# Finish of the recurrent heads, small loads of the attention, and last rows of the last head: one change to a decoder layer step

## The chip, the cores and the metric

The kernel runs on one core of one Trainium2 chip. The metric is the device time of one execution in microseconds. Three runs of the kernel before took 2062.02, 2064.7 and 2070.59 us (median 2064.7).

## What is computed

One step of one decoder layer for 1024 prompt tokens and 32 sample tokens (8 sequences of 4), all in fp32. The part around the change, cut from the reference:

```python
o_att = attend(q, k4, v, lam)                                   # 4 heads of differential attention
o_att = (_rmsnorm(o_att, lp['g_subln']) * (1.0 - lam_init)).reshape(b, t, D_ATT)
y, wkv = _wkv_scan(wkv0.astype(f32), r_h, w_h, k_h, v_h, kk, a_h)   # 8 recurrent heads of 64
mean = jnp.mean(y, axis=-1, keepdims=True)
var = jnp.mean(jnp.square(y - mean), axis=-1, keepdims=True)
y = ((y - mean) * lax.rsqrt(var + GN_EPS)).reshape(b, t, D_RWKV)
y = y * lp['ln_x_w'].astype(f32) + lp['ln_x_b'].astype(f32)
bonus = jnp.sum(r_h * k_h * lp['r_k'].astype(f32), axis=-1, keepdims=True) * v_h
y = (y + bonus.reshape(b, t, D_RWKV)) * g
mix = jnp.concatenate([o_att.astype(x.dtype), o_rwkv], axis=-1) @ lp['w_o']
```

In the attention each head has two maps of scores; `softmax(first) - lam * softmax(second)` weighs the values. The samples attend to 1024 cached keys in 8 pages, found through a page table, and to their own new keys. After `mix` come norms, residuals, a convolutional feed-forward part and a gated embedding, none of them touched here.

## The kernel before

The program is a row of stages, each a block in which every engine has its own list of instructions; engines order themselves by semaphores, and all meet at the end of a block. The stages: the projection and preparation, the transitions of the recurrence (to 648 us), the scan of the recurrence (`rwkv_scan`, to 681), the attention (`attend`, to 942), the finish of the recurrent heads (`finish_rows`, to 1015), and the tail with the remaining products (`tail`, to the end).

**The scan** also loads q and k of head 0 (`ap_dup`) and splits them into a high and a low part (`ap_qs`, `ap_kh`, `ap_kl`) for the attention.

**The attention** walks over 32 steps `s` (4 heads of 8 query blocks of 128, P = 128, U = 32, NQ = 8); the order on each engine is written out in its loop over `s`. A step scores block `s` (`ap_sc`, L865 to L869), takes maxima on VectorE (L1016), exponentials on ScalarE (L1133), weighs the two maps (L1034), turns the weights with block `s - 2` (L893, kept by L1142) and multiplies by the values with block `s - 3` (L905; it leaves PSUM by L1152 and L1154). The eight sample sequences `n` run beside, one in four steps: their scores in three groups (L935), the combination of the two maps by a small matrix (`as_combs`, L951, after the sample's exponential L1191 and the products L1055 to L1062) and the values (L964). SP issues all loads: the page table, `ap_vin` (a head's values), `as_qkv`, `as_mask` and `as_comb` at the block's start, then the 16 pages of sequence 0 (each looked up in the table in SBUF, then loaded), then q and k of the next head at `s % 8 == 0`. These are rounded to the high part on ScalarE in steps 3 to 6 of a head (`split`, L1109) and the low parts made on VectorE in steps 4 to 7 (`low`, L1006, L1009).

After a head's last block its 8 blocks of rows (`ap_orow`) are normed: a root on ScalarE (`root_rows`, L1162), a reciprocal and a product on VectorE (`norm_rows`, L1040, L1042), transposes on TensorE (`turn_rows`, L913), a copy with the gain (`keep_rows`, L1171) and a store (L782). For the last head that follows the last step, and the samples' rows (`as_rows_out`, L1096, L995, L1100) are normed with it: one root over both.

**The finish** works on four pairs `p` of heads (128 rows: two heads of 64, by 1056 tokens). A mean is a product with a block matrix (`blk64`, 1/64 in two 64x64 blocks), which leaves the mean in every row; three matmuls of 352 columns each make a triple. Then the subtraction (`centre`, L1726), the square (L1688), the variance by the same matrix (L1679), root (L1694), reciprocal (L1730), product (L1732), scale and add (L1735, with bonus and bias; the bias is added before by GpSimd, L1771), and GpSimd multiplies by the gate (L1776). The result is rounded to a high part on ScalarE (L1698), and VectorE takes the low part (L1740). Beside it the attention's rows are split into high and low (`o_high` L1702, `o_low` L1744), and two tiles of the output weights (L1718, L1760).

**The tail** starts with matmuls of `Mh`, `Ml` with those weights (L2096).

Of the kernel before, what the change touches and what calls it, by code (L numbers as in the profile page):

```python
# [17 lines left out]
F32 = mybir.dt.float32  # L18
# [692 lines left out]
def attend(kit, a, proj, oT, ident, identb, causal, lam, eps, g_subln, dup, qs, kh, kl):  # L711
# [12 lines left out]
    names = ("table_in", "small_in", "q_zeroed", "q_placed", "w_zeroed", "v_turned", "v_kept", "scored", "moved", "peaked",  # L724
             "biased", "exped", "inverted", "scaled", "combined", "turned", "kept", "summed", "squared", "evacuated", "v_in", "normed",
# [4 lines left out]
    with ExitStack() as ctx:  # L730
        vin = kit.sb(ctx, "ap_vin", [P, SEQ])
# [11 lines left out]
        table = kit.sb(ctx, "as_table", [1, NB * PAGES], I32)  # L743
        qkv = kit.sb(ctx, "as_qkv", [P, 3, HEADS, NS])
        qd = kit.sb(ctx, "as_qd", [P, NB, HEADS, 32])
        vnew = kit.sb(ctx, "as_vnew", [NS, HEADS, P])
        mask = kit.sb(ctx, "as_mask", [P, NB * NS], BF16)
        comb = kit.sb(ctx, "as_comb", [P, 18])
# [17 lines left out]
        def _(sp):  # L766
# [8 lines left out]
            def load_v(h):  # L775
                if h:
                    sp.wait_ge(S["v_turned"], h)
                sp.dma_start(vin[:], proj[h + 2 * HEADS][:, 0:SEQ]).then_inc(S["v_in"], 16)

            def store(h):  # L780
                sp.wait_ge(S["o_kept"], h + 1)
                sp.dma_start(oT[h][:, 0:SEQ], out[:]).then_inc(S["o_stored"], 16)  # L782
# [17 lines left out]

            sp.dma_start(table[:], a["table"]).then_inc(Z["table_in"], 16)
            load_v(0)
            for j in range(3):
                sp.dma_start(qkv[:, j], proj[j * HEADS:(j + 1) * HEADS, :, SEQ:T].rearrange("h p t -> p h t"))\
                    .then_inc(Z["small_in"], 16)
            sp.dma_start(mask[:], a["new_mask"]).then_inc(Z["small_in"], 16)
            sp.dma_start(comb[:, 0:17], a["comb"]).then_inc(Z["small_in"], 16)
            sp.wait_ge(Z["table_in"], 16)
# [3 lines left out]
            for s in range(U + 3):  # L812
                h, n = s // NQ, s // 4
                if s % NQ == 0 and h + 1 < HEADS:
# [12 lines left out]
            store(HEADS - 1)  # L827
            sp.wait_ge(Z["out_kept"], 1)
            sp.dma_start(oT.rearrange("h p t -> p h t")[:, :, SEQ:T], out_s[:]).then_inc(Z["stored"], 16)
            sp.wait_ge(Z["stored"], 16)  # L830
            sp.wait_ge(S["o_stored"], 16 * HEADS)

        @block.gpsimd
        def _(pool):
            nc.gpsimd.memset(qd[:], 0.0).then_inc(Z["q_zeroed"], 1)
            nc.gpsimd.memset(wS[:], 0.0).then_inc(Z["w_zeroed"], 1)
            pool.wait_ge(Z["small_in"], 16 * 5)
# [2328 lines left out]
```

## Time and profile before

| | |
|---|---|
| median of 3 runs | 2064.7 us |
| the profiled execution | 2063.8 us, span 2062.0 us |
| TensorE matmul, weight load | 1852.0 us (90%), 1752.3 us (85%) |
| VectorE, ScalarE, GpSimd | 1078.5 us (52%), 810.7 us (39%), 292.7 us (14%) |
| granted TensorE clock, mean | 0.938 |

The span runs from the first to the last instruction; the execution's own time has 1.8 us around it. Busy time is time in which an engine executes; where several matmuls overlap their ends are modelled. In a row of the trace the number in brackets is how long the engine sat idle before, and the arrow names what it was waiting for. The granted clock is a share of 2.4 GHz: 0.50 is the lower of TensorE's two levels.

### The profile page before, as it was taken

To read this page: it belongs to the slowest core of one execution; us is meant where nothing else is said; L and a number is where in the kernel's file an instruction comes from. 1 tells how busy PE (TensorE), PEld (TensorE's weight loads), DVE (VectorE), ACT (ScalarE), POOL (GpSimd) and SP (SyncE) were. 2 spreads that over 40 slices of the span, in tenths; PEclk is the share of its full clock that TensorE was granted. 3 is DMA by queue.
4 is the path that set the end of the run, shared out by engine and by line. 5 is a ranking of instruction groups with operands and counts; after the bars stand their busy time and mean duration, and the time that the engine had idled before them with its cause. 6 is when DMAs were issued, how large, how long until landed. Compare 5 with 4: busy or idle time off the path is not lost.

```text
span 2062.0 us, 45942 instructions
## 1 busy us (share of the span) xinstructions
PE 1852.0 (90%) x19468; PEld 1752.3 (85%) x19468; DVE 1078.5 (52%) x1790; ACT 810.7 (39%) x1438; POOL 292.7 (14%) x292
## 2 busy tenths in 40 slices
PE   5999999699998588884397999999999999999996
PEld 5988888599997466662397999999999999999996
DVE  4355544345445455545736577553337766532654
ACT  4242323022232266652234554543335555432442
POOL 0011111059971000002100000000000000000000
PEclk9999999899999688886699999999999999999997
DMA  4233333530012677534133343323434422333442
GB/s 153 99 124 128 132 119 135 194 110 3 3 26 45 192 215 196 152 103 169 41 103 134 104 144 129 100 89 118 137 113 153 146 92 93 99 111 106 121 139 95
DMA packets 100140, 240.71 MB, mean 117 GB/s; under 512 B 14243, under 2 KB 18467, under 8 KB 99651
## 3 DMA queue, kind: packets, MB, share of 16 engines
q1 hardware_dynamic: 99362, 235.63, 35.9%
q8 instruction: 154, 2.52, 0.5%
q10 hardware_dynamic: 576, 2.16, 0.3%
q14 instruction: 48, 0.39, 0.1%
HBM read 189.54 MB, written 48.21 MB: 115 GB/s over the span
## 4 chain that ended last, share of the span: by engine, by line
PE 47%; DVE 2%; ACT 1%; issue 1%; DMA 0%; POOL 0%; SPq 0%; ACTq 0%; DVEq 0%
PE tl_acc L2096 45%; PE tl_ple L2096 1%; PE tl_wide L2070 0%; PE tl_wide L2061 0%; DVE tl_tmp L2369 0%; DVE tl_gated L2431 0%; DVE tl_gated L2434 0%; ACT tl_sq_e L2108 0%; ACT tl_wh L2245 0%; DVE tl_Y L2351 0%; DVE tl_Y L2342 0%; ACT tl_Hh L2214 0%; DVE tl_acc_e L2275 0%; DMA tl_xt<-dram_xT 0%; ACT tl_Y L2194 0%
## 5 line engine op out<-in xcount | busy, mean ns | idle before, releaser
L2096 PE MATMUL tl_acc<-tl_Hh,tl_wh 128*128 128x264 f32 x1536 | 438.5, 285 | 7.4 <-DVE tl_Hl L2373 7.4
L2096 PE MATMUL tl_acc<-tl_Hh,tl_wl 128*128 128x264 f32 x1536 | 438.1, 285 | 0.0
L2096 PE MATMUL tl_acc<-tl_Hl,tl_wh 128*128 128x264 f32 x1536 | 436.1, 284 | 0.0
L2415 DVE TENSOR_TENSOR tl_wl<-tl_raw,tl_wh 128x1024 fp32r<-128x1024 f32 (+2 forms) x182 | 206.0, 1132 | 418.7 <-ACT tl_wh L2245 418.5
L2245 ACT ACTIVATE tl_wh<-tl_raw 128x1024 fp32r<-128x1024 f32 (+2 forms) x182 | 178.9, 983 | 497.1 <-PE tl_acc L2096 455.9
L2096 PEld LDWEIGHTS tl_acc<-tl_Hh,tl_wh 128*128 128x128 f32 x1536 | 290.0, 189 | 8.7 <-DVE tl_Hl L2373 8.4
L2096 PEld LDWEIGHTS tl_acc<-tl_Hl,tl_wh 128*128 128x128 f32 x1536 | 290.3, 189 | 0.0
L2096 PEld LDWEIGHTS tl_acc<-tl_Hh,tl_wl 128*128 128x128 f32 x1536 | 290.1, 189 | 0.0
L2096 PE MATMUL tl_acc<-tl_Gl,tl_wh 128*128 128x264 f32 x704 | 200.4, 285 | 0.0
L2096 PE MATMUL tl_acc<-tl_Gh,tl_wl 128*128 128x264 f32 x704 | 200.3, 284 | 0.0
L2096 PE MATMUL tl_acc<-tl_Gh,tl_wh 128*128 128x264 f32 x704 | 200.1, 284 | 0.0
L2289 DVE SCALAR_TENSOR_TENSOR tl_c<-tl_u,par,tl_c 128x528 f32<-128x528 f32 (+1 forms) x176 | 136.6, 776 | 13.2 <-ACT tl_c L2161 6.6
L2096 PEld LDWEIGHTS tl_acc<-tl_Gh,tl_wl 128*128 128x128 f32 x704 | 132.7, 189 | 0.0
L2096 PEld LDWEIGHTS tl_acc<-tl_Gh,tl_wh 128*128 128x128 f32 x704 | 132.6, 188 | 0.0
L2096 PEld LDWEIGHTS tl_acc<-tl_Gl,tl_wh 128*128 128x128 f32 x704 | 132.5, 188 | 0.0
L2698 PE MATMUL fr_ps<-fr_Hh,fr_wh 128*128 128x272 f32 x416 | 124.0, 298 | 5.7 <-DVE fr_wl L2821 5.7
L2821 DVE TENSOR_TENSOR fr_wl<-fr_raw,fr_wh 128x512 fp32r<-128x512 f32 x52 | 37.0, 714 | 175.1 <-ACT fr_wh L2733 175.1
L2698 PE MATMUL fr_ps<-fr_Hl,fr_wh 128*128 128x272 f32 x416 | 121.4, 292 | 0.0
L2698 PE MATMUL fr_ps<-fr_Hh,fr_wl 128*128 128x272 f32 x416 | 121.1, 291 | 0.0
L2451 POOL COPY tl_u<-tl_carry 128x2 f32<-128x2 f32 x88 | 34.5, 392 | 603.3 <-DVE tl_conv_out L2293 355.3
L2733 ACT ACTIVATE fr_wh<-fr_raw 128x512 fp32r<-128x512 f32 x52 | 32.6, 629 | 204.0 <-PE fr_ps L2682 127.6
L2096 PE MATMUL tl_acc<-Mh,tl_wh 128*128 128x264 f32 x256 | 75.1, 293 | 28.4 <-PEq L82 27.7
(360 smaller groups left out, 4458.2 us busy)
## 6 DMA issues: line engine op xcount, KB each, us to landing
tl_raw<-dram_w_up SPq DMA_DIRECT2D x88, 512.0 KB, 3.6
as_kT<-dram_k_pool SPq DMA_DIRECT2D x64, 256.0 KB, 3.1
as_vp<-dram_v_pool SPq DMA_DIRECT2D x64, 256.0 KB, 3.0
tl_raw<-dram_w_down SPq DMA_DIRECT2D x32, 448.0 KB, 3.4
dram_projT<-fr_cur SPq DMA_DIRECT2D x26, 528.0 KB, 2.9
fr_raw<-dram_w_in SPq DMA_DIRECT2D x52, 256.0 KB, 3.6
tl_raw<-dram_w_pg SPq DMA_DIRECT2D x32, 320.0 KB, 3.2
ap_dup<-dram_projT SPq DMA_DIRECT2D x16, 512.0 KB, 8.9
```

The costliest lines, as they stand in the source:

```text
L2096: last = nc.tensor.matmul(out[:, n, 0:HP], w[:, u % 2, k, :], z, start=(begin and q == 0), stop=(end and q == 2))
L2245: nc.scalar.activation(wh[:, u % 2, 0:kt], raw[:, u % 3, 0:kt], ACT.Copy).then_inc(S["rounded"], 1)
L2289: stt(c, uu[:, k:k + n], tap(f"cw{k}", m), c, ALU.mult, ALU.add).then_inc(S[f"tap{k}"], 1)
L2415: tt(wl[:, u % 2, 0:kt], raw[:, u % 3, 0:kt], wh[:, u % 2, 0:kt].bitcast(F32), ALU.subtract).then_inc(S["residued"], 1)
L2451: ins = nc.gpsimd.tensor_copy(uu[:, 0:2], carry[:, x.m])
L2698: last = nc.tensor.matmul(accB[:, n, 0:w2b], w[:, u % 2, k, :], x[:, row, at:at + w2b], start=(row == 0 and q == 0), stop=(row == KD - 1 a ...
L2733: nc.scalar.activation(wh[:, u % 2], raw[:, u % 3], ACT.Copy).then_inc(S["rounded"], 1)
L2821: tt(wl[:, u % 2], raw[:, u % 3], wh[:, u % 2].bitcast(F32), ALU.subtract).then_inc(S["residued"], 1)
```

## The change

Four things are changed.

1. In the finish the variances are no longer spread over all 128 rows at once. A matrix `var_cols` (128x32 for each pair) sums the squares into 2 of 32 rows, all four pairs accumulate into the same rows, and the three groups of 352 tokens stand at rows 0, 32 and 64 of one PSUM bank. One root and one reciprocal work on 96x352. A matrix `var_rows` then spreads the result over the 128 rows, pair by pair, and the product reads it in PSUM. The means have two PSUM tiles instead of one. The bias moves from GpSimd to ScalarE. The loads of the attention's rows all come before bonus and gate, and VectorE's list is in another order.
2. The averaging matrix, the two new ones, and the attention's table, `qkv`, mask, `comb` and first values are loaded in the scan, behind that stage's own loads; SP waits for them there.
3. In the attention q and k of head 1 are loaded ahead of the pages of sequence 0, and the rounding and the low parts of q and k each run one step earlier in every head.
4. At the end of the attention the samples' rows have a root, reciprocal and product of their own; the last head's rows are normed as 7 blocks and 1 block, and stored so; the samples' rows are stored first.

```diff
 # rwkv_scan, SP
             sp.dma_start(yt[:], ysd.rearrange("t h a v -> t (h a v)")).then_inc(S["sample_in"], 16)
+            for dst, src in early:
+                sp.dma_start(dst, src).then_inc(S["early_in"], 16)
+            sp.wait_ge(S["early_in"], 16 * len(early))
             sp.wait_ge(S["state"], NCH)
...
 # attend, VectorE and ScalarE
-                if s % NQ >= NQ - 4 and s // NQ + 1 < HEADS:
-                    low(s // NQ + 1, s % NQ - (NQ - 4))
-            norm_rows(HEADS - 1)
+                if NQ - 5 <= s % NQ < NQ - 1 and s // NQ + 1 < HEADS:
+                    low(s // NQ + 1, s % NQ - (NQ - 5))
+            dve.wait_ge(Z["rooted"], 1)
+            nc.vector.reciprocal(rms[:, 2], rms[:, 2]).then_inc(Z["o_inverted"], 1)
...
+            norm_rows(HEADS - 1)
...
+            norm_rows(HEADS)
...
-                if h < HEADS and NQ - 5 <= i < NQ - 1:
-                    if i == NQ - 5:
+                if h < HEADS and NQ - 6 <= i < NQ - 2:
+                    if i == NQ - 6:
...
+                if s == U + 1:
+                    act.wait_ge(Z["squared"], NB)
+                    nc.scalar.activation(rms[:, 2], rms[:, 2], ACT.Sqrt, bias=eps, scale=1.0 / P).then_inc(Z["rooted"], 1)
+                    root_rows(HEADS - 1)
...
+            root_rows(HEADS)
             keep_rows(HEADS - 1)
+            act.wait_ge(S["o_turned"], HEADS + 1)
+            nc.scalar.activation(out[:, SEQ - P:SEQ], pv[:, 0:P], ACT.Copy, scale=gs[:]).then_inc(S["o_kept"], 1)
...
 # finish_rows, TensorE
+            def var(p):
+                pe.wait_ge(S["squared"], p + 1)
+                for n in range(3):
+                    last = nc.tensor.matmul(pr[group(n), 0:T3], var_cols[:, p, :], sq[:, p % 2, n * T3:(n + 1) * T3],
+                                            start=(p == 0), stop=(p == NPAIR - 1), skip_group_check=True)
+                last.then_inc(S["var"], 1)
+
+            def spread(p):
+                if p >= 2:
+                    pe.wait_ge(S["scaled"], p - 1)
+                for n in range(3):
+                    last = nc.tensor.matmul(wide[p % 2][:, n, 0:T3], var_rows[group(n), p, :], rstd[group(n), :],
+                                            start=True, stop=True)
+                last.then_inc(S["spread"], 1)
+
             mean(0)
+            mean(1)
             for p in range(NPAIR):
-                if p + 1 < NPAIR:
-                    mean(p + 1)
...
+                var(p)
+                if p + 2 < NPAIR:
+                    mean(p + 2)
+            pe.wait_ge(S["inverted"], 1)
+            pe.wait_ge(S["centred"], NPAIR)
+            for p in range(NPAIR):
+                spread(p)
...
 # finish_rows, VectorE and GpSimd
-                dve.wait_ge(S["rooted"], p + 1)
-                nc.vector.reciprocal(sd[:, p % 2], sd[:, p % 2]).then_inc(S["inverted"], 1)
-                dve.wait_ge(S["inverted"], p + 1)
-                tt(dev[:, p], dev[:, p], sd[:, p % 2], ALU.mult).then_inc(S["divided"], 1)
+                dve.wait_ge(S["spread"], p + 1)
+                tt(part(dev[:, p]), part(dev[:, p]), wide[p % 2][:, :, 0:T3], ALU.mult).then_inc(S["scaled"], 1)
...
-            for p in range(NPAIR):
-                pool.wait_ge(bon_in[p], 16)
-                nc.gpsimd.tensor_scalar(BON[:, p], BON[:, p], param("ln_b", 4)[:, p:p + 1], None, ALU.add)\
-                    .then_inc(S["shifted"], 1)
```

How instructions stand on SP around the start of the attention. `wkv_prompt` is the scan's last store, `as_kT` a page of keys, `ap_dup` q and k of a head, `rn_yt` a load of the scan. Before:

```order
L1486 DMA rn_yt<-dram_ysd 32x512
L1488 DMA dram_wkv_prompt<-rn_states 128x256
L1470 UNCONDITIONAL_BRANCH
L765 UNCONDITIONAL_BRANCH
L801 DMA as_table<-dram_table 1x64
L778 DMA ap_vin<-dram_projT 128x1024
L804 DMA as_qkv<-dram_projT 128x4x32 x3
L806 DMA as_mask<-dram_new_mask 128x256
L807 DMA as_comb<-dram_comb 128x17
L785 TENSOR_LOAD as_table
L785 ISA x2
L791 ISA
```

And in the changed kernel, from the scan's last own load to the first look-up of a page:

```order
L1492 DMA ap_vin<-dram_projT 128x1024
L1492 DMA as_table<-dram_table 1x64
L1492 DMA as_qkv<-dram_projT 128x4x32 x3
L1492 DMA as_mask<-dram_new_mask 128x256
L1492 DMA as_comb<-dram_comb 128x17
L1492 DMA rf_blk<-dram_blockmean 128x128
L1492 DMA rf_cols<-dram_var_cols 128x128
L1492 DMA rf_rows<-dram_var_rows 128x512
L1495 DMA dram_wkv_prompt<-rn_states 128x256
L1474 UNCONDITIONAL_BRANCH
L760 UNCONDITIONAL_BRANCH
L768 DMA ap_dup<-dram_projT 64x2x1024 x4
```

The small loads stand before the scan's store; the attention's list begins with the four loads of head 1, and the look-ups of the pages follow them.

VectorE in the finish, from the end of the first subtractions (`rf_dev` the deviations, `rf_sd` the spread root, `Ml` a low part). Before:

```order
L1726 TENSOR_TENSOR rf_dev<-mixed,rf_pm 128x1056 x2
L1744 TENSOR_TENSOR Ml<-rf_O,Mh 128x1056
L1730 RECIPROCAL rf_sd<-rf_sd 128x1056
L1732 TENSOR_TENSOR rf_dev<-rf_dev,rf_sd 128x1056
L1735 SCALAR_TENSOR_TENSOR rf_dev<-rf_dev,par,rf_BON 128x1056
L1726 TENSOR_TENSOR rf_dev<-mixed,rf_pm 128x1056
L1744 TENSOR_TENSOR Ml<-rf_O,Mh 128x1056
L1730 RECIPROCAL rf_sd<-rf_sd 128x1056
```

Now, from the third subtraction's low part on (`rf_rstd` the narrow rows, `rf_wide` the spread ones in PSUM):

```order
L1778 RECIPROCAL rf_rstd<-rf_rstd 96x352
L1764 TENSOR_TENSOR Ml<-rf_O,Mh 128x1056
L1752 TENSOR_TENSOR rf_dev<-rf_dev,rf_wide 128x1056
L1755 SCALAR_TENSOR_TENSOR rf_dev<-rf_dev,par,rf_BON 128x1056
L1752 TENSOR_TENSOR rf_dev<-rf_dev,rf_wide 128x1056
L1755 SCALAR_TENSOR_TENSOR rf_dev<-rf_dev,par,rf_BON 128x1056
L1768 TENSOR_TENSOR tl_wl<-tl_raw,tl_wh 128x1024
L1760 TENSOR_TENSOR Ml<-mixed,Mh 128x1056
L1752 TENSOR_TENSOR rf_dev<-rf_dev,rf_wide 128x1056
L1755 SCALAR_TENSOR_TENSOR rf_dev<-rf_dev,par,rf_BON 128x1056
L1768 TENSOR_TENSOR tl_wl<-tl_raw,tl_wh 128x1024
L1760 TENSOR_TENSOR Ml<-mixed,Mh 128x1056
```

All four subtractions now stand ahead of the one reciprocal, and the residues of the weights and the low parts stand between the scalings instead of behind them.

## Rows read from the trace of the kernel before

**Rows 1.** Windows; busy us (count) of PE, PEld, DVE, ACT, POOL; clock, DMA share, GB/s.

```profile
681.00:942.00 261.00, 196.94 (x1748) 159.82 (x1748) 132.85 (x304) 142.76 (x351) 3.26 (x10) 0.79 0.60 171
942.00:1015.00 73.00, 24.11 (x49) 12.97 (x49) 58.61 (x26) 18.67 (x18) 24.31 (x8) 0.59 0.29 112
...
718.00:720.00 2.00, 1.94 (x6) 1.66 (x7) 0.61 (x2) 2.00 (x8) 0.00 (x0) 0.50 1.05 386
```

**Rows 2.** Timeline, VectorE in the finish: start, us, engine, line, operation [idle before].

```profile
949.89 1.25 DVE L1726 TENSOR_TENSOR rf_dev<-mixed,rf_pm 128x1056 f32<-128x1056 f32 x1 [14.64 <-PE rf_pm L1667]
...
958.46 6.75 DVE L1730 RECIPROCAL rf_sd<-rf_sd 128x1056 f32<-128x1056 f32 x1 [1.01 <-ACT rf_sd L1694]
...
966.54 1.32 DVE L1735 SCALAR_TENSOR_TENSOR rf_dev<-rf_dev,par,rf_BON 128x1056 f32<-128x1056 f32 x1
...
968.94 2.67 DVE L1744 TENSOR_TENSOR Ml<-rf_O,Mh 128x1056 fp32r<-128x1056 f32 x1
...
1008.93 4.75 DVE L1740 TENSOR_TENSOR Ml<-mixed,Mh 128x1056 fp32r<-128x1056 f32 x4
```

**Rows 3.** Timeline, TensorE in the finish and at the tail's start.

```profile
945.96 3.89 PE L1667 MATMUL rf_pm<-mixed,rf_blk 128*128 128x352 f32 x6 [9.46 <-DMA rf_blk<-dram_blockmean]
...
954.83 1.94 PE L1679 MATMUL rf_pq<-rf_sq,rf_blk 128*128 128x352 f32 x6
...
1014.87 0.56 PE L2096 MATMUL tl_acc<-Mh,tl_wh 128*128 128x264 f32 x1 [27.74 <-PEq L82]
```

**Rows 4.** Timeline, ScalarE and GpSimd in the finish: a square, a gating.

```profile
951.18 1.08 ACT L1688 ACTIVATE rf_sq<-rf_dev 128x1056 f32<-128x1056 f32 x1 [13.53 <-DVE rf_dev L1726]
...
968.01 2.48 POOL L1776 TENSOR_TENSOR mixed<-rf_dev,rf_G 128x1056 f32<-128x1056 f32 x1 [4.52 <-DVE rf_dev L1735]
```

**Rows 5.** Timeline, end of the attention to the finish's first issue.

```profile
928.48 1.28 ACT L1162 ACT_TABLE_LOAD   x1
...
931.55 1.22 DVE L1096 TENSOR_TENSOR as_rows_out<-as_rows_out,ap_rms 128x1024 f32<-128x1024 f32 x1
...
932.82 1.97 PE L995 MATMUL ap_sc<-ident,as_rows_out 128*128 128x128 f32 x8 [5.11 <-DVE as_rows_out L1096]
...
934.58 1.92 PE L913 MATMUL ap_tp<-ident,ap_orow 128*128 128x128 f32 x8
...
936.54 1.11 ACT L1171 ACTIVATE ap_out<-ap_tp,ap_gs 128x1024 f32<-128x1024 f32 x1 [6.45 <-PE ap_tp L913]
...
938.05 0.43 SPq L829 DMA_DIRECT2D dram_oT<-as_out  x1
942.08 0.35 SPq L1652 DMA_DIRECT2D rf_blk<-dram_blockmean  x1
```

**Rows 6.** Loads of q and k and their first users, scan and attention.

```profile
648.10 3.12 SPq L1485 DMA_DIRECT2D ap_dup<-dram_projT  x4
...
L1516 ACT ACTIVATE ap_qs<-ap_dup x2: 1041/1049/1057, 660.9 to 661.8; 128x1024 fp32r<-128x1024 f32 x2
...
681.13 0.25 SPq L801 DMA_DIRECT2D as_table<-dram_table  x1
...
691.25 1.16 PE L935 MATMUL as_one<-as_kT,as_qd 128*32 128x384 f32 x8 [0.40 <-DVE as_vnew L1085]
...
716.17 1.06 ACT L1109 ACTIVATE ap_qs<-ap_dup 128x1024 fp32r<-128x1024 f32 x1 [14.91 <-DMA ap_dup<-dram_projT]
...
718.06 0.80 PE L865 MATMUL ap_sc<-ap_kh,ap_qs 128*128 128x512 f32 x1 [10.64 <-ACT ap_pexp L1133]
```

**Rows 7.** Timeline, TensorE at the first head change and in head 1.

```profile
739.97 0.45 PE L865 MATMUL ap_sc<-ap_kh,ap_qs 128*128 128x128 f32 x1 [4.06 <-DVE ap_kl L1009]
...
742.61 3.69 PE L951 MATMUL as_one<-as_combs,as_prob 128*128 128x16 f32 x18
...
766.70 0.54 PE L865 MATMUL ap_sc<-ap_kh,ap_qs 128*128 128x512 f32 x1 [2.14 <-ACT ap_pexp L1133]
...
771.57 2.12 PE L951 MATMUL as_one<-as_combs,as_prob 128*128 128x16 f32 x18 [1.40 <-DVE as_combs L1062]
```

More of the change, by code:

```diff
@@ L799, in values @@
                         .then_inc(Z["v_in"], 16)
[L801 to L808, printed above, removed]
+            load_qk(1)
             for g in range(3):
@@ L813, in _ @@
                 h, n = s // NQ, s // 4
[L814 removed]
+                if s % NQ == 0 and 0 < h and h + 1 < HEADS:
                     load_qk(h + 1)
@@ L911, in turn_rows @@
                 pe.wait_ge(S["kept"], min(NQ * (h + 1) + 3, U))
-                for n in range(NQ):
+                for n in range(NQ if h < HEADS - 1 else NQ - 1):
                     last = nc.tensor.transpose(tp[:, n, :], orow[:, h % 2, n, :], ident)
@@ L1624, in store, with finish_rows @@
         sp.wait_ge(state_out, 32)
-def finish_rows(kit, a, spill, oT, epsg, param, Y, Mh, Ml, raw, wh, wl):
+def finish_rows(kit, a, spill, oT, epsg, param, Y, Mh, Ml, raw, wh, wl, blk64, var_cols, var_rows):
     nc = kit.nc
-    names = ("blk_in", "mean", "centred", "squared", "var", "rooted", "inverted", "divided", "shifted", "affine", "gated", "high", "low",
+    names = ("mean", "centred", "squared", "var", "rooted", "inverted", "spread", "scaled", "shifted", "affine", "gated", "high", "low",
              "o_high", "o_low", "rounded", "residued")
@@ L1706, in _ @@
             square(1)
-            root(0)
             o_high(1)
-            root(1)
             square(2)
             o_high(2)
-            root(2)
             square(3)
-            o_high(3)
-            root(3)
+            act.wait_ge(S["var"], NPAIR)
+            nc.scalar.activation(rstd[0:ROWS], pr[0:ROWS, 0:T3], ACT.Sqrt, bias=epsg[0:ROWS]).then_inc(S["rooted"], 1)
+            o_high(HEADS - 1)
+            for p in range(NPAIR):
+                shift(p)
             for u in range(2):
@@ L1748, in _ @@
             o_low(0)
-            scale(0)
             centre(2)
             o_low(1)
-            scale(1)
             centre(3)
             o_low(2)
+            dve.wait_ge(S["rooted"], 1)
+            nc.vector.reciprocal(rstd[0:ROWS], rstd[0:ROWS]).then_inc(S["inverted"], 1)
+            o_low(3)
+            scale(0)
+            scale(1)
+            residue(0)
+            low(0)
             scale(2)
-            o_low(3)
+            residue(1)
+            low(1)
             scale(3)
-            for u in range(2):
-                dve.wait_ge(S["rounded"], u + 1)
-                tt(wl[:, u], raw[:, u], wh[:, u].bitcast(F32), ALU.subtract).then_inc(S["residued"], 1)
-            for p in range(NPAIR):
-                low(p)
-            dve.wait_ge(S["residued"], 2)
+            low(2)
+            low(3)
             dve.wait_ge(S["low"], NPAIR)
             dve.wait_ge(S["o_low"], HEADS)
+            dve.wait_ge(S["residued"], 2)
         @block.gpsimd
         def _(pool):
-            for p in range(NPAIR):
-                pool.wait_ge(bon_in[p], 16)
-                nc.gpsimd.tensor_scalar(BON[:, p], BON[:, p], param("ln_b", 4)[:, p:p + 1], None, ALU.add)\
-                    .then_inc(S["shifted"], 1)
             for p in range(NPAIR):
@@ L3101 @@
     i = np.arange(C)
+    var_cols = np.zeros((P, NPAIR, 32), np.float32)
+    var_rows = np.zeros((P, NPAIR, P), np.float32)
+    for p in range(NPAIR):
+        for h in range(2):
+            var_cols[h * C:(h + 1) * C, p, 2 * p + h] = 1 / C
+            var_rows[2 * p + h::32, p, h * C:(h + 1) * C] = 1.0
     lev = [(j[:, None] == i[None, :]) | ((j[:, None] >> (n + 1) == i[None, :] >> (n + 1))
```

128 lines of the change are left out of this document (70 added, 58 removed).

## The prediction

> **What bounds the kernel now.** I read the page first (TensorE busy nine tenths almost everywhere), then busy time by stage, then the instructions in order of time in the slack stages. The attention [rows 1] keeps TensorE 197 of 261 us busy at a mean granted clock of 0.79; the finish keeps it 24 of 73 us busy at 0.59. Every tail matmul stands behind the finish, which ends at the first tail matmul [rows 3]: what the finish or the attention loses comes off the end one for one.
>
> In the finish VectorE sets the time: it is busy 58.6 of 73 us [rows 1]. A reciprocal over 1056 elements takes 6.75 us [rows 2], and there are four: 27 us, with TensorE waiting behind them. Before that, 3.9 us pass from the block's first DMA issue [rows 5] to the first matmul, which waits for the averaging matrix [rows 3].
>
> In the attention I looked for what ended last before each long TensorE wait. 10.64 us are lost before block 5 of head 0, where ScalarE sat 14.91 us on the loads of head 1's q and k [rows 6]; 4.06 us at each of the three head changes, for the last low part of k [rows 7].
>
> **The change part by part.**
>
> *Finish, until the scaling can begin.* The block's start is t = 0 (942.1). The matrices are loaded in the scan, so the first mean runs at 0. A mean triple takes 3.9 us at the low clock; six such halves take 1.94 at the high one [rows 3]. Now two means come first, then variance and mean alternate: eight triples. I take two at the low clock (3.6 each) and five more by the 1.9 of rows 3 up to the third variance, 16.7; the last mean is done at 14.8, its subtraction (1.25) [rows 2] and square (1.08) [rows 4] at about 17.3, the last variance at 19. One square root over 96x352 replaces four over 1056 (at most the 1.08 of the square), and one reciprocal over 352 takes 6.75 x 352/1056 = 2.25. With two hand-overs the first spread matmuls start at about 21 if the narrow matmuls of 32 columns or rows share the array and the root is short, 24 if they don't. Bounds: 18.5 (clock up early, narrow ones nearly free) and 33 (all eight triples at 3.6, root, reciprocal, spread at the low clock). I take 21.
>
> The narrow matmuls of different column groups may run side by side. The Trainium skill ("TensorEngine Tiling (Array Packing)", Key Properties) says that different tiles work in parallel, but that changing the tiling mode drains the array; the finish changes it seven times. By the drain the chain would be longer by an estimated 7 x 0.3 to 0.6 us, 2 to 4 us (half a matmul of rows 3 to a whole one), and the sum would give back as much. No row here isolates that.
>
> *Finish, from there on.* VectorE has four products with the spread rows (one input in PSUM, 1.25 as the subtraction), four scale-and-adds (1.32), two weight residues (below 1.2, as one of the four low parts), four low parts (4.75/4 = 1.19) [rows 2]: 17.4 us. GpSimd has four gatings of 2.48 [rows 4]. A subtraction from SBUF took 2.67 instead of about 1.2 while a gating ran: it began at 968.94 and ended 1.1 us after the gating did [rows 2, 4]. So I put these operations one after the other, and only the products beside a gating. The order then gives, from the start of scaling: gating 0 to 5.2, scale-and-add 1 to 6.5, residue 0 to 7.6, gating 1 to 10.1, low 0 to 11.2, scale 2 to 13.8, residue 1, gating 2 and low 1 to 18.5, scale 3 to 21.0, low 2 to 22.2, gating 3 to 24.7, its rounding on ScalarE (1.08) and low 3 to 27.0. If they ran side by side, 21.4.
>
> The Trainium skill ("SBUF — State Buffer", SBUF: two separate sides) calls this an exclusive lock, taken also by a VectorE operation with two SBUF inputs, so by the scale-and-add, which no row shows beside a gating. Without it for that one the end would be 25.8 instead of 27.0.
>
> The adding of the bias moves from GpSimd (four) to ScalarE, four more at about 1.08; ScalarE is free from the root to the first gating. It is priced at nothing; should the bias or bonus loads, now behind all four attention loads in SP's queue, land after 21, scaling waits as long. The finish ends at 21 + 27.0 + 1.2 (end of the low parts to first tail matmul) [rows 2, 3] = 49.2 against 72.8 now: **23.6 us less** (11.6 to 31.7).
>
> *End of the attention.* The table load (1.28), the root, and the product of the samples' rows (1.22) now come before the last block has left, and only one block of eight is late. After 928.48 there remain: sample transposes (1.97), seven head transposes (7/8 of 1.92), copy (about 1.0), the last block's copy, SP's issue. The sample rows are stored first. I get the last issue at about 933.9 instead of 938.05 [rows 5]; the landing stays. The added wait for the samples' sums stands before the last block's square on ScalarE, and its sums are due before that. **4.2 us less** (2.5 to 5.5).
>
> *Start of the attention.* Eight small loads leave SP's queue; three more go into the scan with them. There SP waits for all of them; behind it stands only the state store, due 27 us later, so nothing. At the start, head 1's q and k (four loads, 2 MB) are now ahead of the sample pages. In the scan such loads took 660.9 - 648.1 = 12.8 us from issue to use [rows 6]. From the block's first issue at 681.13 [rows 6] that is 693.9. The first three pages (each 128x512 fp32, together 0.79 MB) at 386 GB/s [rows 1] take 2 us: the first sample scores start at 696 instead of 691.25. The order from there to block 5 is the old one (16.2 us to 707.4) plus a rounding on ScalarE and a low part on VectorE that come a step earlier, 1.2: block 5 at 713.4 instead of 718.06, **4.6 us less**. If pages overlap with the q and k loads, 7; if they land 3 us later still, 1.5.
>
> *Low parts one step earlier.* Score 8 no longer waits 4.06 us, but the next thing, the sample combination, needs the sample exponential: its matmuls at 742.61 move only to about 740.8, **1.8 us** at each of three changes. In heads 1 and 2 the earlier rounding lands between a root and an exponential that TensorE waits 2.14 us for, and the earlier low part before a combination it waits 1.40 us for [rows 7]: 1.1 + 1.0 us lost, twice. Net 1.2. If the clock then holds over the change, sample matmuls cost 2.12 instead of 3.69 [rows 7] and the value matmuls behind them gain as much: up to 3 more each. I take **3 us** (-2 to 10).
>
> **Sum.** 23.6 + 4.2 + 4.6 + 3 = 35.4. The profiled execution took 2063.8 us (span 2062.0); the median of the runs is 2064.7, 0.9 above. 2063.8 - 35.4 = **2028 us**.
>
> **The rivals.**
> *More than that:* the clock rises early and stays up over the head changes, and VectorE and GpSimd wait little. 28 + 10 + 5 + 5 = 48: 2016. For it: the gaps that let the clock fall to 0.5 shrink. Against: the 1.4 us wait for the combination stays.
> *The finish becomes bound by TensorE:* eight triples, the roots and the spread all at the low clock, and pages stuck behind q and k. 11.6 + 4.2 + 0 + 1 = 17: 2047. For it: the clock was low in the finish until 954.83 [rows 3]. Against: the triples now follow without the reciprocals between.
> *It doesn't do what it says:* the reciprocal's time doesn't shrink with its columns, or each is as late as before; under 10 us gained, about 2056.
> *Slower:* the clock in the attention. There is now one wait of nearly 10 us at its start, and TensorE is busy 197 us at a mean 0.79 [rows 1]. Were the mean to fall to x, its work would grow by 197 x (0.79/x - 1) us; from x = 0.67 that eats the 35 us, and at 0.64 the kernel takes 2028 + 46 = 2074. For it: at 718 to 720, right after the 10.64 us wait, the clock is at 0.50 [rows 1, 6]. Against: of the waits, 10.6 and 4.06 three times go.
>
> **How the numbers follow.** Forecast, 2020 to 2038: 0.62. More: 0.14. TensorE-bound finish: 0.18. Not what it says: 0.03. Slower: 0.03. The 8-in-10 range takes in parts of both neighbours: 2016 to 2042. About 0.5% (10 us) is what a measurement here tells from no change: faster 0.93, same 0.04, slower 0.03.
>
> **What would show it.** One reciprocal of about 2.25 us in the finish; its first matmul right at the block's start; 48 to 50 us from there to the first tail matmul; scale-and-adds or low parts of about 2.5 us beside the gatings. No wait of ScalarE on head 1's loads, but TensorE idle until about 696; score 8 with no wait on the low part. Last store issued some 4 us earlier, relative to the last block. The tail's length unchanged within 3 us: if not, the cause is one I did not name. The forecast is wrong if the finish takes over 60 us or the attention doesn't shorten.

## The result, and the profile after

The changed kernel took 2033.99 us (median of four runs, 2029.61 to 2034.84) against 2064.23 us in the runs of before beside it: a ratio of 0.984, 95% interval 0.982 to 0.987. Forecast were 2028 us and a range of 2016 to 2042. The profiled execution took 2033.6 us with a span of 2031.7, so 30.3 us less span than before, where the sum of the terms said 35.4. Cut by the same marks in both traces (first load of the scan, first score matmul of the attention, first DMA issue of the finish, first tail matmul):

| stage | before | after | change | forecast |
|---|---|---|---|---|
| up to the scan's first load | 648.10 | 646.39 | -1.7 | 0 |
| scan | 33.08 | 35.28 | +2.2 | 0 |
| attention | 260.90 | 254.08 | -6.8 | -11.8 |
| finish | 72.79 | 47.26 | -25.5 | -23.6 |
| tail | 1047.13 | 1048.69 | +1.6 | 0 |

Busy time by stage, the answer to [rows 1] (windows of the changed kernel: us, then busy us and count of PE, PEld, DVE, ACT, POOL, then granted clock, DMA share, GB/s):

```profile
681.62:935.75 254.13, 199.44 (x1748) 159.66 (x1748) 133.63 (x307) 143.51 (x354) 3.27 (x10) 0.81 0.59 173
935.75:983.01 47.26, 19.26 (x73) 8.62 (x73) 34.67 (x23) 19.27 (x19) 12.25 (x4) 0.61 0.44 171
```

VectorE's work in the finish fell from 58.6 to 34.7 us. The attention keeps TensorE busy 2.5 us longer than before at about the same clock: what it won, it won in waits.

The finish instruction by instruction, which answers to [rows 2 to 4] (timeline of the changed kernel: start, us, engine, line, operation, idle before and its releaser):

```profile
935.79 6.54 PE L1675 MATMUL rf_wide<-mixed,rf_blk 128*128 128x352 f32 x12 [5.04 <-PEq L82]
...
942.26 0.79 PE L1682 MATMUL rf_pr<-rf_sq,rf_cols 128*32 128x352 f32 x6
942.98 2.04 PE L1675 MATMUL rf_wide<-mixed,rf_blk 128*128 128x352 f32 x6
...
951.03 0.55 ACT L1734 ACTIVATE rf_rstd<-rf_pr,epsc 96x352 f32<-96x352 f32 x1 [0.90 <-PE rf_pr L1682]
951.62 2.35 DVE L1778 RECIPROCAL rf_rstd<-rf_rstd 96x352 f32<-96x352 f32 x1 [1.44 <-ACT rf_rstd L1734]
...
954.02 2.72 PE L1690 MATMUL rf_wide<-rf_rstd,rf_rows 32*128 32x352 f32 x12 [3.04 <-DVE rf_rstd L1778]
...
955.63 1.25 DVE L1752 TENSOR_TENSOR rf_dev<-rf_dev,rf_wide 128x1056 f32<-128x1056 f32 x1 [0.55 <-PE rf_wide L1690]
...
958.15 1.25 DVE L1752 TENSOR_TENSOR rf_dev<-rf_dev,rf_wide 128x1056 f32<-128x1056 f32 x1
958.39 2.46 POOL L1799 TENSOR_TENSOR mixed<-rf_dev,rf_G 128x1056 f32<-128x1056 f32 x1 [273.29 <-DVE rf_dev L1755]
959.44 2.52 DVE L1755 SCALAR_TENSOR_TENSOR rf_dev<-rf_dev,par,rf_BON 128x1056 f32<-128x1056 f32 x1
...
969.14 3.25 POOL L1799 TENSOR_TENSOR mixed<-rf_dev,rf_G 128x1056 f32<-128x1056 f32 x1 [3.78 <-DVE rf_dev L1755]
970.04 3.46 DVE L1760 TENSOR_TENSOR Ml<-mixed,Mh 128x1056 fp32r<-128x1056 f32 x1
...
980.61 1.26 DVE L1760 TENSOR_TENSOR Ml<-mixed,Mh 128x1056 fp32r<-128x1056 f32 x1 [3.41 <-ACT Mh L1715]
983.01 0.56 PE L2119 MATMUL tl_acc<-Mh,tl_wh 128*128 128x264 f32 x1 [22.01 <-PEq L82]
```

One reciprocal of 2.35 us stands where four of 6.75 were, and the first mean no longer waits for a load. A scale-and-add beside a gating takes 2.52 instead of 1.32 us, a low part 3.46 instead of 1.25. From the first product (955.63) to the last low part's end it is 26.2 us.

The end of the attention, the answer to [rows 5] (timeline of the changed kernel):

```profile
925.26 1.28 ACT L1215 ACT_TABLE_LOAD   x1
...
927.45 0.37 ACT L1149 ACTIVATE ap_sq<-ap_pv,ap_small 128x128 f32<-128x128 f32 x1 [0.40 <-PE ap_pv L895]
...
928.41 1.09 PE L984 MATMUL ap_sc<-ident,as_rows_out 128*128 128x128 f32 x8 [1.00 <-DVE as_rows_out L1091]
...
929.65 0.99 PE L903 MATMUL ap_tp<-ident,ap_orow 128*128 128x128 f32 x7 [0.15 <-DVE ap_orow L1034]
...
930.48 0.27 PE L988 MATMUL ap_pv<-ident,ap_orow 128*128 128x128 f32 x1
...
932.08 0.43 SPq L819 DMA_DIRECT2D dram_oT<-ap_out  x1
935.75 0.32 SPq L1661 DMA_DIRECT2D rf_O<-dram_oT  x1
```

The table load is done before the last block's square (927.45), and the transposes run at the full clock (granted 1.00 from 928.40 to 931.20; before, 0.50 from 932.82 to 936.50): 1.09 us, and 0.99 for seven blocks, instead of 1.97, and 1.92 for eight. From that square to the finish's first issue it is 8.3 us; before, it was 14.3: issue at 942.08 [rows 5], and this square (timeline of the kernel before):

```profile
927.75 0.37 ACT L1152 ACTIVATE ap_sq<-ap_pv,ap_small 128x128 f32<-128x128 f32 x1 [2.21 <-PE ap_pv L905]
```

The start of the attention and the first head change, the answers to [rows 6, 7] (timeline of the changed kernel):

```profile
681.62 2.56 SPq L768 DMA_DIRECT2D ap_dup<-dram_projT  x4
685.46 8.07 SPq L786 DMA_DIRECT2D as_kT<-dram_k_pool  x8
...
696.08 1.51 PE L924 MATMUL as_one<-as_kT,as_qd 128*32 128x384 f32 x8 [10.04 <-DMA as_kT<-dram_k_pool]
...
710.63 3.81 PE L940 MATMUL as_one<-as_combs,as_prob 128*128 128x16 f32 x18 [4.24 <-DVE as_combs L1055]
715.25 0.77 PE L854 MATMUL ap_sc<-ap_kh,ap_qs 128*128 128x512 f32 x1
...
737.82 3.82 PE L940 MATMUL as_one<-as_combs,as_prob 128*128 128x16 f32 x18 [1.74 <-DVE as_combs L1055]
...
763.65 0.64 PE L854 MATMUL ap_sc<-ap_kh,ap_qs 128*128 128x512 f32 x1 [3.09 <-ACT ap_pexp L1130]
...
769.91 3.13 PE L940 MATMUL as_one<-as_combs,as_prob 128*128 128x16 f32 x18 [2.69 <-DVE as_combs L1055]
```

The long wait at the start is now for the key pages (10.04 us), not for ScalarE. The sample combination waits at the start (4.24), at the head change (1.74) and in the middle of head 1 (2.69; before, 1.40 [rows 7]).

### The profile page after: what moved, and what is told of

Read it like the earlier page. It is cut to its first block, busy times and chain, and to the rows that moved or that the text cites. A ratio compares the mean times of both kernels' runs of the same rounds, so it can differ in the third digit from the quotient of the medians.

```text
span 2031.7 us, 45987 instructions
## 1 busy us (share of the span) xinstructions
PE 1849.8 (91%) x19492; PEld 1748.4 (86%) x19492; DVE 1051.9 (52%) x1790; ACT 812.5 (40%) x1442; POOL 280.9 (14%) x288
## 3 DMA queue, kind: packets, MB, share of 16 engines
q8 instruction: 154, 2.52, 0.5%
## 4 chain that ended last, share of the span: by engine, by line
PE 48%; DVE 2%; ACT 1%; issue 1%; POOL 0%; ACTq 0%; DVEq 0%
PE tl_acc L2119 46%; PE tl_ple L2119 1%; PE tl_wide L2084 1%; PE tl_wide L2093 1%; ACT tl_wh L2268 0%; DVE tl_tmp L2392 0%; ACT tl_sq_e L2131 0%; DVE tl_gated L2454 0%; DVE tl_gated L2457 0%; DVE tl_Y L2374 0%; DVE tl_Y L2365 0%; ACT tl_Hh L2237 0%; DVE tl_acc_e L2298 0%; ACT tl_Y L2217 0%; ACT tl_sq_x L2131 0%
## 5 line engine op out<-in xcount | busy, mean ns | idle before, releaser
L2705 PE MATMUL fr_ps<-fr_Hh,fr_wh 128*128 128x512 f32 x208 | 85.7, 412 | 14.2 <-DVE fr_Hl L2944 14.2
```

Of the source, the lines that this page charges most:

```text
L2705: last = nc.tensor.matmul(accA[:, t % 2, :], w[:, u % 2, k, :], x[:, row, 0:W_A], start=(row == 0 and q == 0), stop=(row == KD - 1 and q = ...
```

## The experiments

Single stages are compared by their traces, one for each run, with the marks of the table above. "Turn n" is the first matmul that uses the combination of sample n; turns 1, 3 and 5 follow a head change, 2, 4 and 6 lie in the middle of a head. The medians of the runs alone don't settle 3 us: the part ahead of the scan, the same code in all these kernels, took 646.4 to 656.9 us in the profiled executions. The kernel before took 2062.85 us (median) beside the first four kernels, 2064.63 beside the next four, and 2064.3 beside the rest.

**The finish alone.** The attention of before; in the scan only the finish's three matrices as early loads.

```
-            early = [(vin[:], proj[2 * HEADS][:, 0:SEQ]), (table[:], a["table"])]
...
+            early = [(blk64[:], a["blockmean"]), (var_cols[:], a["var_cols"]), (var_rows[:], a["var_rows"])]
...
-                   table, qkv, mask, comb, vin)
```

> The changed kernel's finish on the attention of before; of the early loads only the finish's three matrices are in the scan. Theory (the finish's gain is its own, and the scan's 2.2 us come from the clock at its start, not from the loads): finish, block's first issue to first tail matmul, 47.3 +-1.5 us; attention 261 +-1.5; scan 33 to 36 whatever the loads; about 2038 to 2040 us in all. Rival A (the finish is short because TensorE comes out of the changed attention at a higher clock): finish 50 us or more. Rival B (the seven loads of the attention's small inputs slow the scan): scan 33.0, as before.

Measured: finish 47.42, attention 261.54, scan 34.04 us; 2037.15 us, ratio 0.987 (0.985 to 0.989). The finish's gain is its own and needs nothing of the rest. On the scan, rival B falls: three early loads gave 34.04, and another kernel with all ten (keys first, below) 34.21. In these traces the scan's length goes with the granted clock over its first 33 us, which hold 516 matmuls (513 in the last row):

| kernel | early loads | clock | scan, us |
|---|---|---|---|
| before | 0 | 0.90 | 33.08 |
| finish alone | 3 | 0.84 | 34.04 |
| keys first | 10 | 0.84 | 34.21 |
| changed | 10 | 0.79 | 35.28 |
| changed, run again | 10 | 0.74 | 36.08 |

The traces show where the changed kernel's 2.2 us arise. The scan's first three steps take 2.10 us instead of 1.67, at a granted clock of 0.50 (649.60 to 653.80; before, 1.00 from 651 to 654): 1.3 us. The matmuls are slow from 648.51 on (1.12 us for sixteen instead of 0.68), and the first early load is issued only at 650.36, so the loads did not bring the clock down. Behind that the steps meet GpSimd's low part of q at another moment: the update of the state on VectorE, 0.42 us alone, takes 2.11 us beside it, and the one that met it before took 1.06. That is another 1.1 us. The two engines in the scan (timelines of the kernel before, then of the changed one):

```profile
662.02 4.85 POOL L1522 TENSOR_TENSOR ap_qs<-ap_dup,ap_qs 64x1024 fp32r<-64x1024 f32 x2 [56.21 <-ACT ap_qs L1516]
...
663.60 1.06 DVE L1546 TENSOR_TENSOR rn_states<-rn_tsum,ELC 128x256 f32<-128x256 f32 x1
```

```profile
660.50 4.84 POOL L1529 TENSOR_TENSOR ap_qs<-ap_dup,ap_qs 64x1024 fp32r<-64x1024 f32 x2 [56.40 <-ACT ap_qs L1523]
...
661.02 2.11 DVE L1553 TENSOR_TENSOR rn_states<-rn_tsum,ELC 128x256 f32<-128x256 f32 x1
```

Why the clock at the scan's start is lower in one execution than in another stays open; of the kernel before there is only one trace.

**The low parts at their old steps.**

```
-                if NQ - 5 <= s % NQ < NQ - 1 and s // NQ + 1 < HEADS:
-                    low(s // NQ + 1, s % NQ - (NQ - 5))
+                if NQ - 4 <= s % NQ and s // NQ + 1 < HEADS:
+                    low(s // NQ + 1, s % NQ - (NQ - 4))
...
-                    high(h, i - (NQ - 6))                 # steps 2 to 5
+                    high(h, i - (NQ - 5))                 # steps 3 to 6
```

> The changed kernel with the rounding and the low parts of the next head's k back at their old steps. My prediction: this costs 3 us (attention 257). Theory from the changed kernel's trace (what the heads gain at a change they lose again in the middle of a head, where the sample combination now comes after a low part): attention 252 to 254, that is up to 2 us faster than the changed kernel; the wait of a score matmul for the low part at a head change is back at about 4 us, and the sample combination's matmul in the middle of heads 1 and 2 comes some 29 us after the one before it instead of 32.1 and 31.1.

Measured: attention 251.37 us, 2.7 less than in the changed kernel (2032.94 us). The timeline of this kernel, the head change and head 1:

```profile
737.09 0.44 PE L854 MATMUL ap_sc<-ap_kh,ap_qs 128*128 128x128 f32 x1 [4.07 <-DVE ap_kl L1000]
...
764.78 0.50 PE L854 MATMUL ap_sc<-ap_kh,ap_qs 128*128 128x512 f32 x1 [2.14 <-ACT ap_pexp L1130]
...
769.65 3.81 PE L940 MATMUL as_one<-as_combs,as_prob 128*128 128x16 f32 x18 [2.39 <-DVE as_combs L1055]
```

The 4.07 us wait is back, yet turn 0 to turn 1 is only 0.9 us longer (28.07 against 27.19): behind the low part the combination was the next wait anyway. From turn 1 to turn 2 it is 2.2 us shorter (29.93 against 32.09), from 3 to 4 1.2 us; from 5 to 6 it is 1.1 us longer, and turn 0 comes 1.2 us earlier. So the old step is not 3 us dearer. One trace is weak for 2.7 us: the changed kernel run again (below) took 253.14. Taken over all traces here without another spacing of the low parts, the stretch from block 5's score to the last block's square is 208.6 to 210.7 us in the four with the old step (the kernel before, the finish alone, this one, and the three edits together; mean 209.7) and 210.3 to 212.6 in the six with the earlier one (mean 211.7). My term for the shift had the wrong sign: the earlier step costs some 2 us there.

**Key pages ahead of q and k.**

```
-            load_qk(1)
             for g in range(3):
                 keys(0, g)
+            load_qk(1)
             values(0)
```

> The changed kernel with the loads of head 1's q and k behind the first sample's three groups of key pages, ahead of its value pages. Theory (loads are served in the order of their issue, so what the first sample scores wait for is the 2 MB of q and k ahead of them): first sample scores 5 to 8 us after the block's first issue instead of 14.5; ScalarE then waits for q and k, some 5 us later than now; block 5's score 30 to 33 us after the block's first issue instead of 33.6, attention 251 to 254. Rival (16 DMA engines share the bandwidth, so the order of issue is worth little): first sample scores within 2 us of where they are now, block 5's score within 1 us, attention 254 +-1.

Measured: first sample scores after 6.2 us, as the theory had it; but block 5 after 36.0 us (33.6 in the changed kernel) and attention 256.25, longer by 2.2, which neither had. 2035.33 us. Its timeline:

```profile
688.19 8.07 SPq L786 DMA_DIRECT2D as_kT<-dram_k_pool  x8
696.30 2.83 SPq L768 DMA_DIRECT2D ap_dup<-dram_projT  x4
...
710.65 1.06 ACT L1106 ACTIVATE ap_qs<-ap_dup 128x1024 fp32r<-128x1024 f32 x1 [11.83 <-DMA ap_dup<-dram_projT]
```

What the theory left out are SP's issues: eight key pages take SP 8.07 us (1.0 each, the page number being read from a table first), so q and k are issued 8 us late. ScalarE starts on them 14.35 us after their first issue, and has waited 11.83 us, with everything behind it. The bytes count too: in the scan of the kernel before it was 12.8 us from issue to use [rows 6].

**The gatings on VectorE.**

```
+                dve.wait_ge(g_in[p], 16)
+                dve.wait_ge(S["affine"], p + 1)
+                tt(Y[:, p], dev[:, p], G[:, p], ALU.mult).then_inc(S["gated"], 1)
...
-                nc.gpsimd.tensor_tensor(Y[:, p], dev[:, p], G[:, p], ALU.mult).then_inc(S["gated"], 1)
```

(The second weight residue moves behind the last gating.)

> The changed kernel with the four gatings on VectorE instead of GpSimd. Theory (a gating on GpSimd and a VectorE operation of SBUF inputs shut each other out, so that a gating costs the finish its whole 2.5 us): VectorE's 18 operations from the first product on follow without a stretched one, 22.3 us from the first product to the end of the last low part instead of 26.2; finish 43 to 44 us. Rival (the two engines share SBUF only in part, and a stretched low part hides a gating): VectorE's added 4 x 1.2 us come on top of the low parts' unstretched times, 26 us or more, finish 47 us or more.

Measured: finish 43.59 us, 22.56 from the first product to the last low part; 2030.68 us. From its timeline, a gating, a low part and the last two:

```profile
967.99 1.26 DVE L1759 TENSOR_TENSOR mixed<-rf_dev,rf_G 128x1056 f32<-128x1056 f32 x1
...
979.23 1.25 DVE L1763 TENSOR_TENSOR Ml<-mixed,Mh 128x1056 fp32r<-128x1056 f32 x1
...
985.41 2.42 DVE L1763 TENSOR_TENSOR Ml<-mixed,Mh 128x1056 fp32r<-128x1056 f32 x2
```

With GpSimd silent nothing is stretched: four more operations on VectorE, and the stage is 3.7 us shorter. The two engines had taken turns in the changed kernel.

**Head 1's q and k loaded in the scan.**

```
             sp.wait_ge(S["early_in"], 16 * len(early))
+            sp.wait_ge(S["low"], 4)                       # head 0's parts are done with the buffer
+            for n in range(2):
+                ...
+                    sp.dma_start(dup[rows, n], src).then_inc(next_qk, 16)
             sp.wait_ge(S["state"], NCH)
...
-            load_qk(1)                                    # at the attention's start
```

> The changed kernel with the loads of head 1's q and k moved into the scan: SP issues them there as soon as head 0's low parts are done with the buffer, some 9 to 11 us before the attention begins, ahead of the state's store. Theory (at the start the attention loses time to two things on one queue: the 2 MB of q and k ahead of the key pages, and 1.0 us of SP per page): first sample scores 6 to 8 us after the block's first issue (14.5 in the changed kernel), ScalarE never waits for q and k, block 5's score 26 to 29 us after the block's first issue (33.6), attention 247 to 250. Rival (the loads only move: they land as late, or slow the scan's end as much): scan 5 us longer, or first sample scores after 10 us or more and attention 253 to 255.

Measured: first sample scores after 6.0 us, block 5 after 23.8 (33.6 in the changed kernel), attention 244.71; 2028.57 us. The theory was right and too small. Of the rival, half holds: the scan is 37.76 us, 2.5 longer, 2.0 of it since from the issue of the state's store, now behind the four loads, to the first score it is 4.2 us (681.15 to 685.32) instead of 2.2:

```profile
671.64 2.58 SPq L1497 DMA_DIRECT2D ap_dup<-dram_projT  x4
681.15 0.35 SPq L1499 DMA_DIRECT2D dram_wkv_prompt<-rn_states  x1
...
691.36 0.85 PE L923 MATMUL as_one<-as_kT,as_qd 128*32 128x384 f32 x8 [1.09 <-DMA as_kT<-dram_k_pool]
```

**The end of the attention undone.**

```
-                for n in range(NQ if h < HEADS - 1 else NQ - 1):
+                for n in range(NQ):
...
-                if s % NQ == 2 and NQ <= s < U:
+                if s % NQ == 2 and s >= NQ:
                     root_rows(s // NQ - 1)
...
-            norm_rows(HEADS)
...
-            root_rows(HEADS)
```

> The changed kernel with the end of the attention as before: the last head's rows normed in one part, together with the samples'. Theory (the 6.0 us between the last block's square and the finish's first issue are the code's: the table load, the root and the product no longer behind the last block): that stretch is 14.3 us again, attention 260, finish 47.3. My prediction's term: 4.2 us, attention 258.3. Rival (part of the gain is the clock of TensorE, whose sixteen transposes there ran at the low level before and at the high one after): the transposes take 1.0 us each group as in the changed kernel, and the stretch is 12 to 12.5 us.

Measured: the stretch from the last block's square (926.83) to the finish's first issue is 14.28 us again, and the transposes are back at the low clock:

```profile
931.90 1.97 PE L981 MATMUL ap_sc<-ident,as_rows_out 128*128 128x128 f32 x8 [5.11 <-DVE as_rows_out L1082]
933.66 1.91 PE L900 MATMUL ap_tp<-ident,ap_orow 128*128 128x128 f32 x8
```

So all 6.0 us are this edit's. Part of them is the clock, but through the code: TensorE waits 1.00 us ahead of the transposes instead of 5.11, and they take 2.35 us in all instead of 3.88. The attention was 257.05, not 260: from its first score to turn 7 it was 3.0 us shorter without an edit there, so two traces of the same instructions can differ by as much. 2035.46 us.

**Low parts at steps 4, 5, 5 and 6.**

```
+LOW_PARTS = {4: (0,), 5: (1, 2), 6: (3,)}
-                if NQ - 5 <= s % NQ < NQ - 1 and s // NQ + 1 < HEADS:
-                    low(s // NQ + 1, s % NQ - (NQ - 5))
+                for part in LOW_PARTS.get(s % NQ, ()) if s // NQ + 1 < HEADS else ():
+                    low(s // NQ + 1, part)
...
```

(Each rounding stands one step ahead of its low part.)

> The changed kernel with the next head's k and q low parts at steps 4, 5, 5 and 6 of a head instead of 3, 4, 5 and 6, each rounding one step ahead of its low part: no low part in a step in which VectorE also starts a sample's maxima (3 and 7). Theory (a low part costs time only where it stands before the sample combination or before a head's first score): attention 249 to 251, shorter than with parts at 3 to 6 (254) and at 4 to 7 (251.4); between the sample combinations' matmuls 27 to 28 us at a head change and 29.8 to 30 in the middle of heads 1 and 2. Rival (any low part at any step costs its 1.2 us and ScalarE's rounding as much; what differs is only how many come before a combination): 252 to 254.

Measured: attention 242.98 us, 165.4 from turn 1 to turn 7 (174.0 in the changed kernel), at a granted clock of 0.86 there instead of 0.83; 2030.34 us. The attention is shorter than the theory's 249 to 251, and the clock is higher with it; this trace doesn't tell how much of the gain is the order's (the split candidate below bears on it).

**Three edits together:** gatings on VectorE, low parts at the old steps, q and k in the scan (the diffs above).

> The changed kernel with three edits together: gatings on VectorE, low parts at their old steps, head 1's q and k loaded in the scan. Theory (the terms add): attention 244 to 247, finish 43.6, so about 11 to 13 us below the changed kernel: 2021 to 2023 us where the part ahead of the scan takes as long. Rival (the early q and k give the start nothing, since the sample's combination and not ScalarE's wait sets block 5): attention 250 to 252, 2027 us.

Measured: attention 238.99, finish 43.44, scan 38.04; 2020.65 us, ratio 0.979 (0.977 to 0.981). Finish and scan are what the single edits gave. The attention is 3.0 us less than their two gains together leave (254.08 - 2.7 - 9.4 = 242.0) and below the 244 to 247 expected; that surplus is not explained, and it is no more than two traces of the same instructions differed by above.

**The candidates, and the changed kernel beside them.** The first takes the low parts at 4, 5, 5 and 6 and splits the early q and k:

```
             for n in range(2):
+                sp.wait_ge(S["low"], 2 * n + 2)           # q 5 us ahead of k
```

> Gatings on VectorE, low parts at steps 4, 5, 5 and 6, and head 1's q and k loaded in the scan, here q as soon as the low parts of head 0's q are done (5 us earlier) and k when those of k are. Theory: with half of the 2 MB issued 5 us earlier less of it stands ahead of the state's store, so the scan is 1 to 2.5 us shorter than with all four loads behind the last low part (38 us); attention 230 to 235 us, finish 43.4; 2012 to 2018 us. Rival (the attention's 243 us with parts at 4, 5, 5 and 6 was one run's clock and not the order): attention 237 to 240, 2019 to 2022 us.

The second leaves the four loads together:

> As the kernel with the three edits together (gatings on VectorE, q and k of head 1 loaded in the scan behind the last low part), but with the low parts at steps 4, 5, 5 and 6 instead of 4 to 7. Theory (the order of the low parts is worth 8 us wherever it stands): attention 230 to 234 instead of 239.0, from the second sample combination's matmul to the last 165 to 167 us instead of 170; scan 38 us. Rival (one run's clock): attention 237 to 240, those six intervals 169 to 174 us.

And the changed kernel unedited:

> The changed kernel itself, run beside these two for the comparison. Theory (single stages repeat within 1.5 us where the code is the same; the part ahead of the scan wanders by some 10 us): attention 253 to 255.5, finish 47 to 47.6, from the second sample combination's matmul to the last 173 to 174.5 us. Rival (the attention's clock is as free as that of the part ahead of the scan): attention anywhere from 245 to 258.

Measured: 2011.74 (ratio 0.975, 0.973 to 0.977), 2008.48 (0.975, 0.973 to 0.978) and 2033.66 us (0.986, 0.984 to 0.988). Either candidate is 1.1 to 1.2% faster than the changed kernel on the same chip. The changed kernel repeated its stages: attention 253.14, turn 1 to 7 173.8, finish 47.21; its time ahead of the scan did not (656.3). The split kernel's scan took 33.97 us, 4 less than the 38 and not 1 to 2.5 as expected (once more, below, 36.05). Its attention is 244.58 where the unsplit one's is 231.32: the first lies above its theory and its rival, the second is what the theory said. The whole attention in windows, first of the split, then of the unsplit kernel:

```profile
681.32:925.90 244.58, 199.88 (x1748) 160.45 (x1748) 133.82 (x307) 142.44 (x354) 3.22 (x10) 0.80 0.59 171
```

```profile
686.42:917.74 231.32, 189.29 (x1748) 151.60 (x1748) 133.44 (x307) 142.67 (x354) 3.23 (x10) 0.86 0.62 181
```

The same 1748 matmuls take TensorE 199.9 us at a granted clock of 0.80 and 189.3 at 0.86. In the attention both kernels hold the same order on every engine, so the order of the low parts does not by itself give the 165 us from turn 1 to turn 7 (173.4 in the split kernel, 164.2 in the unsplit one).

**The split candidate once more** (no edit).

> The kernel with gatings on VectorE, low parts at 4, 5, 5 and 6, and q and k of head 1 loaded in the scan in two halves, once more. Its attention took 244.6 us, 173.4 of them between the second and the last sample combination's matmul; the two other kernels with low parts at these steps took 165.4 and 164.2 there. Theory (the clock level is settled anew in each execution, also by what the program did long before): this time 163 to 172 us there, attention 231 to 243, and the time follows. Rival (the program sets it: starting 5 us earlier puts the stages of the heads in another phase): 173 +-1 us again, attention 244 to 245.

Measured: 172.6 us from turn 1 to turn 7, attention 242.69; 2012.8 us, with runs from 2006.7 to 2023.7 at mean clocks between 0.944 and 0.952. The profile stands by the rival, and the spread of the runs by the theory. The unsplit candidate's five runs spread as widely, 2006.95 to 2019.78 us at mean clocks between 0.945 and 0.954, so neither program holds one clock. Why the higher clock came in two traces with this order and not in the two others stays open.

## Why the prediction came out

**Finish (forecast -23.6, measured -25.5).** The first spread matmul began 18.3 us after the block's start (954.02), forecast 21 and just under the lower bound of 18.5: the first two means took 6.54 instead of 7.2 us, and the narrow variances 0.79 each. The first product followed 1.6 us later, at 19.9; for the spread's own time the sum had no term. From there to the end of the last low part it took 26.2 us, forecast 27.0, by the alternation of VectorE and GpSimd that one subtraction of [rows 2, 4] had suggested; the VectorE-only variant confirmed it. The whole finish, 47.26 us, came in under the 48 to 50 that were to show it. What the single parts of this change are worth, the rows tell and no run: none undoes one of them by itself.

The Trainium skill ("SBUF — State Buffer", SBUF: two separate sides) gives the lock also to a VectorE operation with two SBUF inputs, and the trace agrees: the scale-and-add took 2.52 us beside a gating, 1.32 alone, while the product with one input in PSUM kept its 1.25 (958.15).

The Trainium skill ("TensorEngine Tiling (Array Packing)", Key Properties) has the array drain at each change of mode. If it does here, it costs nothing that these rows resolve: the six narrow matmuls of 0.79 us from 942.26 are followed by the next means at 942.98.

The rival of a finish bound by TensorE fell with it: means after the first two took 2.04 us a triple, at the high clock (granted 1.00 from 942.98 to 951.00).

**End of the attention (forecast -4.2, measured -6.0).** The mechanism was right. Mis-sized were the transposes: I put them at 1.97 and 7/8 of 1.92 us, and they took 2.35 together, where the engine's wait in front of them had shrunk from 5.11 to 1.00 us. That is 1.3 of the 1.8 us.

**Start (forecast -4.6, measured -3.3).** "The first sample scores start at 696" held (696.08), and so did the missing ScalarE wait. The order from there to block 5 took 19.2 us and not 17.4: the combination waited 4.24 us, for which there was no term. The 17.4 holds 1.2 us for the earlier rounding and low part; the old-step kernel came to block 5 after 32.4 us, 1.2 sooner, but so did the kernel with the end undone (32.5), which has the earlier step. The eight small loads that the working takes off SP's queue are seven in the listing; nothing in the sum hangs on it.

**Low parts a step earlier (forecast -3, measured some +2 behind block 5, six traces against four; +2.7 for the whole attention by the old-step kernel alone).** This is the step that failed. "1.8 us at each of three changes" was 0.9 to 1.2; "1.1 + 1.0 us lost, twice" was 2.2 and 1.2; and the part that made the term positive, that "the clock then holds over the change", did not happen: the sample matmuls of turn 1 still take 3.82 us, and the mean clock from turn 1 to turn 7 is 0.83 in the changed kernel, 0.83 before and 0.82 with the old step.

**What was put at nothing.** The scan lost 2.2 us and the tail 1.6, the part ahead of the scan gave 1.7. The scan lost it to the clock of its first steps and to one state update held up by GpSimd (above). The tail took 1044.3 to 1048.8 us over all these kernels with the same code, so its 1.6 us lie inside what it does by itself.

Summed: 35.4 us were forecast and 30.3 came. From block 5 to the last block's square the attention is 2.5 us longer than before where 3 less were forecast (5.5); the start gave 1.3 less, and the scan, the tail and the part ahead of them cost 2.1. The finish gave 1.9 and the end of the attention 1.8 more than forecast. That the time lies well inside the range is in part luck: a term of the wrong sign was partly made up by two that were taken too small.

## What to carry to other kernels

A moved instruction is worth what the next wait behind it leaves: look up what else the waiting engine will need, and what now stands in front of another wait, before counting the stall as won. Where two engines block each other, try the work on the faster one, even if it is the busier: here a gating took GpSimd 2.46 us or more and VectorE 1.26, and the finish went from 47.3 to 43.6 us. A buffer that comes free in the stage before is the place to start the next stage's load, with its queue's other transfers counted.

## What the runs showed of the hardware

- SP took 1.0 us to issue a load of a page looked up in a table (8.07 for eight), and 0.64 for a part of q and k with a fixed address (2.56 for four). In the key-first kernel this put the issue of q and k 8 us back. Other loads with a fixed address took SP from 0.28 (`as_table`) to 3.17 us (`as_comb`) in the changed kernel's scan.
- The same instructions in the same order ran at mean granted clocks of 0.80 and 0.86 over a whole attention, 13 us apart, in kernels that differ only in when two of four loads were issued in the stage before.
- VectorE and GpSimd hold each other up in both directions: a gating issued 0.2 us into a weight residue (968.91) took 3.25 us instead of 2.46, and in the scan a state update issued 0.5 us into GpSimd's low part of q took 2.11 us instead of 0.42.
